# A hybrid decoder layer: rows normed per expert block, first loads of the attention issued in the front, and one row tile turned later

## What is computed

```python
mod = jax.nn.silu(c) @ w_ada[l] + b_ada[l]                  # shift, scale, gate, twice
u = x * (1.0 + sc1) + sh1
mix = token_mixer(u, w_in[l], w_conv[l], w_a[l], w_b[l], w_o[l])   # gated conv + stick-breaking attention, 8 heads
x = layer_norm(DN_ALPHA * x + g1 * mix, ln1_g[l], ln1_b[l])
u2 = x * (1.0 + sc2) + sh2
ffn = moe_ffn(u2, w_router, b_router, w_gate[l], w_up[l], w_down[l])   # 16 experts, each token goes to 2
x = layer_norm(DN_ALPHA * x + g2 * ffn, ln2_g[l], ln2_b[l])
```

## Time and profile before

| | value |
|---|---|
| runs, median of 3 (lowest, highest) | 2713.44 us (2708.99, 2715.66) |
| profiled execution, its own time | 2713.14 us |
| its span | 2711.5 us |
| PE, PEld busy | 2491.6 us (92%), 2081.0 us (77%) |
| DVE, ACT, POOL busy | 1443.4 us (53%), 1123.4 us (41%), 842.7 us (31%) |
| mean granted TensorE clock | 0.965 of 2.4 GHz |
| DMA | 548.04 MB, 202 GB/s over the span |
| chain of waits: gate and up products, down products of the experts | 16%, 8% of the span |

### The profile page before, as it was taken

How to read it: one execution, slowest core, us unless ns; L and a number is a source line. 1 busy time by engine, 2 the same in 40 slices (tenths; PEclk the granted TensorE clock), 3 DMA queues, 4 the chain that set the end, 5 groups by cost and what they waited for, 6 DMA issues and landing times. The chain is left out here.

```text
span 2711.5 us, 35984 instructions
## 1 busy us (share of the span) xinstructions
PE 2491.6 (92%) x12505; PEld 2081.0 (77%) x12506; DVE 1443.4 (53%) x1871; ACT 1123.4 (41%) x1846; POOL 842.7 (31%) x692
## 2 busy tenths in 40 slices
PE   5999899999999999999989989994998999999990
PEld 4788678778888888888878877884787888888780
DVE  6122156665656566665654335775446545534755
ACT  3122144554544444454542012212556545534754
POOL 2111023452222222222221345665322222322326
PEclk9999999999999999999999999996999999999995
DMA  7699676767575666585537666532567646555847
GB/s 265 232 312 314 250 231 189 250 199 233 184 224 165 227 186 218 173 270 183 171 122 239 213 182 210 187 117 108 164 180 228 207 135 204 169 145 146 266 122 263
DMA packets 258254, 548.04 MB, mean 202 GB/s; under 512 B 23716, under 2 KB 93464, under 8 KB 257496
## 3 DMA queue, kind: packets, MB, share of 16 engines
q1 hardware_dynamic: 236072, 483.07, 53.7%
q0 software_dynamic: 14720, 45.04, 7.6%
q10 hardware_dynamic: 7344, 18.35, 1.7%
HBM read 393.37 MB, written 153.02 MB: 202 GB/s over the span
## 5 line engine op out<-in xcount | busy, mean ns | idle before, releaser
L93 PE MATMUL mx_acc<-u_u,mx_w_hi 128*128 128x512 f32 x1792 | 571.4, 400 | 1.5 <-DMA mx_w_lo<-halves 1.5
L722 POOL TENSOR_TENSOR mx_wt<-mx_wt,mx_rest 128x127 f32<-128x127 f32 (+15 forms) x128 | 271.5, 2121 | 741.5 <-DVE mx_rest L924 741.5
L93 PEld LDWEIGHTS mx_acc<-u_u,mx_w_hi 128*128 128x128 f32 x1792 | 326.1, 190 | 65.9 <-DMA mx_w_lo<-halves 1.9
L932 DVE TENSOR_TENSOR mx_wt_lo<-mx_p_t,mx_wt_hi 128x512 fp32r<-128x512 f32 (+2 forms) x320 | 192.1, 604 | 326.4 <-ACT mx_wt_hi L887 324.5
L93 PE MATMUL mx_acc<-u_u,mx_w_lo 128*128 128x512 f32 x896 | 352.8, 394 | 0.0
L887 ACT ACTIVATE mx_wt_hi<-mx_p_t 128x512 fp32r<-128x512 f32 (+2 forms) x320 | 170.8, 534 | 405.4 <-PE mx_p_t L774 359.3
L924 DVE TENSOR_TENSOR_SCAN mx_rest<-mx_rest,mx_zero 128x128 f32<-128x128 f32 (+15 forms) x128 | 315.8, 2467 | 8.6 <-ACT mx_wt L869 8.6
L93 PE MATMUL moe_p_gu<-keep_wide_hi,moe_x_hi 128*128 128x512 f32 x656 | 262.6, 400 | 14.1 <-DVE keep_wide_lo L2043 13.0
L93 PE MATMUL moe_p_gu<-keep_wide_hi,moe_x_lo 128*128 128x512 f32 x656 | 258.1, 393 | 0.0
L93 PE MATMUL moe_p_gu<-keep_wide_lo,moe_x_hi 128*128 128x512 f32 x656 | 257.9, 393 | 0.0
L868 ACT ACTIVATE mx_rest<-mx_p_z 128x512 f32<-128x512 f32 (+2 forms) x320 | 171.0, 534 | 100.0 <-PE mx_p_z L761 58.9
(11 more groups left out here) (257 smaller groups left out, 5130.2 us busy)
## 6 DMA issues: line engine op xcount, KB each, us to landing
mx_w_hi<-halves SPq DMA_DIRECT2D x98, 512.0 KB, 3.8
mx_w_lo<-halves SPq DMA_DIRECT2D x98, 512.0 KB, 5.2
keep_stay<-in_w_gate SPq DMA_DIRECT2D x64, 512.0 KB, 5.3
keep_stay<-in_w_up SPq DMA_DIRECT2D x64, 512.0 KB, 6.4
keep_stay<-in_w_down SPq DMA_DIRECT2D x32, 1024.0 KB, 6.7
u_saved<-u_u SPq DMA_DIRECT2D x4, 4096.0 KB, 19.5
mx_w_mod<-in_w_ada SPq DMA_DIRECT2D x64, 256.0 KB, 5.2
gate_t<-mx_g_out SPq DMA_DIRECT2D x64, 256.0 KB, 5.1
```

Source lines behind the costliest of these rows:

```text
L93: mm = pe.matmul(out, a, b, start=first and n == 0, stop=last and n == len(pairs) - 1, skip_group_check=True)
L722: pool.tensor_tensor(wt[:, t % 2, 0:w - 1], wt[:, t % 2, 0:w - 1], rest[:, t % 2, 1:w], ALU.mult).then_inc(m["weights_done"], 1)
L932: dve.tensor_tensor(wt_lo[:, first:first + k - j], p_t[:, n % TR, 0:(k - j) * P].rearrange("p (j t) -> p j t", t=P), f32(wt_hi[:, first:fi ...
```

## The change

Three parts, independent of each other.

**1. The last norm goes into the expert loop.** Per block, the 128 rows of an earlier block are gathered from `acc` by POOL (`gather_rows`), centered by DVE (`center_rows`: two moments of 512 values each, their sum, subtraction of the mean with a product), scaled by ACT (`scale_rows`), given their bias by DVE (`add_bias`), and scattered to `out` by POOL (`store_rows`). Each token is in two blocks, so it is normed and stored twice, and the later store has both experts' contributions. The norm's row has its reciprocal root from POOL in `deviation`. SP's loads of `acc` and ACT's stores at the end are gone. Seven records are kept for five, moved by two copies of 128x12. At the start two blocks' iterations have a `load_clear` in place of the gathered rows; behind the last block the rows of the last three blocks are left.

**2. First loads in the front.** The places of the first head's keys, queries, values and two weight halves (`First`) now lie on front's x, stage and ring, and SP loads them within the front: keys at unit n = 38, queries and values at 39, the second queries at 40, the halves at 41 and 43, with the waits that free these places. The mixer's SP code begins with the remaining keys, two loads of w_ada's rows and the remaining values.

**3. First row tile turned later.** In the step t = 2 of the first norm `turn(0)` stands behind k = 6 and not behind k = 1. The other steps are unchanged.

```diff
+    def load_q(self, sp, n, qk_hi, qk_lo):
+        h, c = divmod(n, 4)
+        cols = slice(c * NB, (c + 1) * NB)
+        for half, src in enumerate((qk_hi, qk_lo)):
+            sp.dma_start(f32(self.q[half * HD:(half + 1) * HD, n % 2]), src[h * HD:(h + 1) * HD, cols]
+                         ).then_inc(self.q_in[n % 2], 16)
+
+    def load_k0(self, sp, h, qk_hi, qk_lo):
+        for half in range(2):
+            rows = slice(half * HD, (half + 1) * HD)
+            for dst, src in ((self.k0_hi, qk_hi), (self.k0_lo, qk_lo)):
+                sp.dma_start(f32(dst[rows, h % 2]), src[AW + h * HD:AW + (h + 1) * HD, 0:NB]
+                             ).then_inc(self.k0_in[h % 2], 16)
+
+    def load_v0(self, sp, h, v_tok):
+        sp.dma_start(f32(self.v0[:, h % 2]), v_tok.rearrange("(j p) h d -> p j h d", p=P)[:, 0:4, h]
+                     ).then_inc(self.v0_in[h % 2], 16)
+
+    def load_halves(self, sp, slot, n, halves):
+        for part, w in enumerate((self.w_hi, self.w_lo)):
+            sp.dma_start(f32(w[:, slot]).rearrange("p k n -> p (k n)"), halves[n, part]
+                         ).then_inc(self.halves_in[slot], 16)
+
```

In front, mixer and first norm:

```diff
+                if n == TB * UNITS - 10:
+                    sp.wait_ge(m["turned"], KD * TB)
+                    for i in range(2):
+                        sp.wait_ge(stored[i], 32 * UNITS)
+                    ahead_of.load_k0(sp, 0, qk_hi, qk_lo)
+                if n == TB * UNITS - 9:
+                    ahead_of.load_q(sp, 0, qk_hi, qk_lo)
+                    ahead_of.load_v0(sp, 0, v_tok)
+                if n == TB * UNITS - 8:
+                    ahead_of.load_q(sp, 1, qk_hi, qk_lo)
+                if n in (TB * UNITS - 7, TB * UNITS - 5):
+                    for i in range(2):
+                        sp.wait_ge(fill_kept[i], 32 * (FRONT_FILL // 2))
+                    slot = 0 if n == TB * UNITS - 7 else 1
+                    ahead_of.load_halves(sp, slot, slot, halves)
...
-            load_k0(0)
-            load_q(0)
-            load_halves(0)
+            load_k(0)
             load_mod(0)
-            load_q(1)
-            load_v0(0)
-            load_halves(1)
-            load_k(0)
             load_mod(1)
             load_v(0)
             for h in range(HEADS):
...
-                    if k == 1:
-                        if t - 3 in LATE_LOGITS:
-                            logits(t - 3)
+                    if k == 1 and t - 3 in LATE_LOGITS:
+                        logits(t - 3)
+                    if k == (KD - 2 if t == 2 else 1):
                         turn(t - 2)
```

GpSimd in the experts' stage (the iteration b with its waits, and the end):

```diff
@@ -1777,36 +1801,60 @@
                     else:
                         sp.wait_ge(m["dn_lo_done"], e * KF + (b - KD))
                     load_piece(sp, e, i, w_gate, w_up, w_down, stay, piece_in)
-            sp.wait_ge(m["gu_lo_done"], E * KD)
-            sp.wait_ge(m["dn_lo_done"], E * KF + KF)
-            sp.wait_ge(m["last_added"], 48)
-            for t in range(NT):
-                sp.dma_start(rows[:, t], acc[t * P:(t + 1) * P, :]).then_inc(rows_in[t], 16)
...
-                    wait_apart(pool, marks["pool"], m["record_ready"], 4 * n + (i + 1))
+                pool.tensor_copy(shifted[:], record[:, 1:SLOTS]).then_inc(m["record_step"], 1)
+                wait_apart(pool, marks["pool"], m["record_step"], n + 1)
+                pool.tensor_copy(record[:, 0:SLOTS - 1], shifted[:]).then_inc(m["record_ready"], 1)
+                wait_apart(pool, marks["pool"], m["record_ready"], n + 1)
...
+            def deviation(n):
+                wait_apart(pool, marks["pool"], m["row_mv"], n)
+                pool.tensor_scalar(var[:, 0:1], mv[:, 0, 1:2], EPS / ALPHA ** 2, None, ALU.add).then_inc(m["row_var"], 1)
+                wait_apart(pool, marks["pool"], m["row_var"], n)
+                pool.tensor_tensor(rstd[:, 0:1], var[:, 0:1], minus_half[:], ALU.pow).then_inc(m["row_rstd"], 1)
 
...
+                if n > 1:
+                    deviation(n - 1)
+                    load_clear(n - 1)
...
-
+            def block_rows(b, c=None):
+
+                if c is not None:
+                    wait_apart(pool, marks["pool"], m["normed"], b + 2)
+                    store_rows(0, row_out, m["out_stored"])
                 wait_apart(pool, marks["pool"], m["y_out"], b * 2 + 6)
-                add_rows(0, y, m["y_added"])
+                wait_apart(pool, marks["pool"], m["row_in"], b * 16 + 48)
+                add_rows(2, m["y_added"])
                 wait_apart(pool, marks["pool"], m["x_turned"], b + 4)
                 gather_x(b + 4)
+                if c is not None:
+                    wait_apart(pool, marks["pool"], m["out_stored"], c * 16 + 16)
+                pool.sem_inc(m["out_free"], 1)
+                deviation(b + 3)
                 wait_apart(pool, marks["pool"], m["y_added"], b * 16 + 16)
                 pool.sem_inc(m["y_free"], 1)
                 wait_apart(pool, marks["pool"], m["x_in"], b * 16 + 80)
                 shift_records(b + 4)
                 load_record(b + 5)
...
+                wait_apart(pool, marks["pool"], m["scaled"], b + 3)
+                gather_rows(1, row_in, m["row_in"])
+                record_known(b + 5)
+
+            block_rows(0)
+            block_rows(1)
+            with pool.Fori(0, total - 4) as c:
+                block_rows(c + 2, c)
+            wait_apart(pool, marks["pool"], m["normed"], total)
+            store_rows(0, row_out, m["last_stored"])
+            wait_apart(pool, marks["pool"], m["y_out"], total * 2 + 2)
+            wait_apart(pool, marks["pool"], m["row_in"], total * 16 + 16)
+            add_rows(2, m["last_added"])
+            pool.wait_ge(m["last_stored"], 16)
+            pool.sem_inc(m["out_free"], 1)
+            deviation(total + 1)
+            pool.wait_ge(m["last_added"], 16)
+            wait_apart(pool, marks["pool"], m["scaled"], total + 1)
+            gather_rows(2, row_in, m["row_in"])
+            gather_rows(3, last_in, m["last_row_in"])
+            wait_apart(pool, marks["pool"], m["normed"], total + 1)
+            store_rows(1, row_out, m["last_stored"])
+            deviation(total + 2)
+            pool.wait_ge(m["last_mv"], 1)
+            pool.tensor_scalar(var[:, 1:2], mv[:, 1, 1:2], EPS / ALPHA ** 2, None, ALU.add).then_inc(m["last_var"], 1)
+            pool.wait_ge(m["last_var"], 1)
+            pool.tensor_tensor(rstd[:, 1:2], var[:, 1:2], minus_half[:], ALU.pow).then_inc(m["last_rstd"], 1)
+            pool.wait_ge(m["last_stored"], 32)
+            pool.sem_inc(m["out_free"], 1)
+            wait_apart(pool, marks["pool"], m["normed"], total + 2)
+            store_rows(2, row_out, m["last_stored"])
+            pool.wait_ge(m["last_stored"], 48)
+            pool.wait_ge(m["last_normed"], 1)
+            store_rows(3, last_out, m["last_stored"])
+            pool.wait_ge(m["last_stored"], 64)
```

ScalarE and VectorE:

```diff
+            def scale_rows(n):
+                act.wait_ge(m["row_rstd"], n + 1)
+                act.wait_ge(m["centered"], n + 1)
+                act.wait_ge(m["out_free"], n + 1)
+                act.activation(row_out, row_in, ACT.Copy, scale=rstd[:, 0:1]).then_inc(m["scaled"], 1)
+
             def body(b, e, first):
                 high_h(b)
                 act.wait_ge(m["gu_used"], b * KD + 2 * KD)
                 for i in range(2):
                     act.activation(act_g[:, i * 256:(i + 1) * 256], p_gu[:, 0, i * 256:(i + 1) * 256], ACT.Silu
                                    ).then_inc(m["silu_done"], 1)
+                scale_rows(b)
                 high_x(b + 1)
...
+            def center_rows(n):
+                dve.wait_ge(m["row_in"], n * 16 + 16)
+                for i in range(2):
+                    dve.bn_stats(stats[:, 0, i], row_in[:, i * NB:(i + 1) * NB]).then_inc(m["row_stats"], 1)
+                wait_apart(dve, marks["dve"], m["row_stats"], 2 * n + 2)
+                dve.bn_aggr(mv[:, 0], stats[:, 0].rearrange("p a b -> p (a b)")).then_inc(m["row_mv"], 1)
+                dve.wait_ge(m["row_mv"], n + 1)
+                dve.scalar_tensor_tensor(out=row_in, in0=row_in, scalar=mv[:, 0, 0:1], in1=ln_g[:], op0=ALU.subtract,
+                                         op1=ALU.mult).then_inc(m["centered"], 1)
+
+            def add_bias(n):
+                dve.wait_ge(m["scaled"], n + 1)
+                dve.tensor_tensor(row_out, row_out, ln_b[:], ALU.add).then_inc(m["normed"], 1)
+
             def body(b, e, first):
                 low_h(b)
                 evict(b)
+                center_rows(b)
                 for i in range(2):
                     w = slice(i * 256, (i + 1) * 256)
                     dve.wait_ge(m["silu_done"], 2 * b + (i + 1))
                     dve.tensor_tensor(h[:, w], p_gu[:, 1, w], act_g[:, w], ALU.mult).then_inc(m["h_done"], 1)
                 low_x(b + 1)
+                add_bias(b)
                 if first:
```

240 lines of the change are left out of this document (91 added, 149 removed).

## The result

The changed kernel takes 2793.67 us (median of 4, 2793.28 to 2794.83) against 2713.78 us of before (median of 4), a ratio of 1.0296 with a 95% interval of 1.0284 to 1.0309: 80 us slower. The forecast was 2783, the range 2740 to 2850. The profiled execution has a span of 2793.1 us against 2711.5, so 81.6 us are to be found in the two traces.

A forecast was written before the change was run, and what follows sets the result against it. TensorE, busy 92% of the span, was taken as the bound, so only its idle stretches count. 23 + 60 + 11 + 14 - 26 - 7.1 - 5.4 = +69.5 us on 2713.14 gave 2783 us, range 2740 to 2850.

The forecast's parts named there:

- The chain: Plain block: turn, gather's issue, variance, power and scale precede x_hi, which starts 4.45 us later against 3.69 of slack.
- The changes: Twelve changes of expert: 3.3 us of idle TensorE plus 1.7 of slow clock each, +60 us (bounds 30 and 72).
- The three others: Three changes behind an expert of one block, where TensorE waits already: 3.6 us each, +11 us.
- the first two steps: Start of the expert loop: root also waits for gather's landing and moved records, +14 us (bounds 6 and 22).
- The plain blocks: 23 steps between blocks without change of expert or start: 1.0 us each, +23 us (bounds nothing and +46).
- the forecast case: Whole kernel: the summed terms, 2783 us, own range 2766 to 2800, chance 0.42.
- the rival of the long round: Expert loop: gathered rows land late, every block waits 2 us more, 80 above forecast less overlap, 2860 us; chance 0.15.
- my two signs of being wrong: Expert loop: x_hi starting within 3 us of the turn, or the block's period set by gathers of `acc`.
- The end: Behind the last blocks: tail norm mostly gone, -26 us (bounds -18 and -32).
- Front: Mixer's start: keys and queries already loaded, first product may begin at 330.6, -7.1 us (-4 to -10).
- First norm: Later `turn(0)`: its 5.72 us of idle is filled, -5.4 us (bounds -2 and -7).
- Contention of VectorE and GpSimd: Each block: centering or bias holds up GpSimd's root by 1.1 us, 44 in all less slack, 2823 us; chance 0.10.

The follow-up runs named there:

- front_turn: The kernel before with parts 2 and 3 of the change, without part 1: 2697.95 us, ratio 0.9950.
- turn_only: The kernel before with part 3 of the change alone: 2711.81 us, ratio 1.0001.
- root_early: The changed kernel with GpSimd's root (and the wait for the last scatter to `out`) ahead of its wait for the turn: 2763.75 us, ratio 1.0198.
- center_late: Changed kernel, scale behind x_hi or, at changes, the second high half (bias likewise), and centering behind h and x_lo except in experts' last blocks: 2743.98 us, ratio 1.0116.
- gather_early: The changed kernel with the gather of the norm's rows from `acc` issued ahead of the record copies and record load: 2843.74 us, ratio 1.0496.

## Why the prediction was right, point by point

- **The chain** behind the turn was as worked out: x_hi 3.97 us behind the turn, where I had 4.5. Of the rows I summed, only the waits were guessed, and too high by half a microsecond (the terms as written add to 2208.5, not 2208.4). For a plain block with its rows in time this left 0.34 us of loss and not 0.8, let alone 1.0.
- **The changes**: with the rows in time 2.81 us idle where I had 3.3, and behind five of these seven 1.4 to 2.9 us of slow clock, behind two none, 1.3 in the mean, where I had 1.7. The twelve came to 71 us and not to 60 because five of them also wait for late rows, which the forecast did not have there. The three others took 9.6 (11), the first two steps 15.0 (14).
- **The plain blocks**: 26 us for 23, nearly as forecast, but of other parts. 17 of them cost 6.6 together, where 17 were forecast; six wait for late rows and cost 19.7, where 6 were.
- **Late rows are the term that the forecast case left out.** They were the rival of the long round, priced 2 us a block for all 40 blocks; the rows came late in eleven blocks, each the second of its expert, and what they cost came on top of the forecast case, not in its place. I had set the two as alternatives, where they add. If these eleven steps had cost what the others of their kind did, the loop would be 36 us shorter, an estimate from the table of steps. Of my two signs of being wrong, x_hi within 3 us of the turn did not show; a period set by the gathers of `acc` did, for these eleven steps of 40.
- **The end**: -28.7 (forecast -26).
- **Front**: `front_turn` and `turn_only` leave 14 us for it (in the profiled executions 9 to 11), where I had 7.1. The first product gained 5.07, two less than forecast: the barrier came 0.9 later, and GpSimd's copy of the identity ends 1.2 us behind the mixer's first load, which I hadn't looked at. But I had missed a second stall of before: its mixer's SP code issues the other keys (L595) behind fourteen other loads, and TensorE waits for them (timeline of before, a row that I hadn't read):

```profile
354.60 0.19 PEld L760 LDWEIGHTS mx_p_z<-mx_k_hi,mx_q 128*128 128x128 f32 x1 [5.15 <-DMA mx_k_lo<-qk_lo]
```

  In after those keys are the first loads of the mixer, and this wait (4.71 us for the product) is gone.
- **First norm**: a step that failed. I had -5.4 with bounds of -2 and -7; measured is -1.2 by the medians (within 0.1% of nothing), as the logits wait 3.18 us. I had named that wait and then left it at almost nothing; the row that sets it, ScalarE's copy behind its scale of the next row tile, does not move with the turn.
- **Contention of VectorE and GpSimd.** In after the root is mostly computed while VectorE has no such instruction, and the variance takes 0.28 (two take 1.20), so the rival that had it as a cost in each block did not come. In `root_early`, where it falls beside the centering, it takes 1.19 (timeline):

```profile
2284.47 1.28 DVE L2125 SCALAR_TENSOR_TENSOR keep_stay<-keep_stay,moe_mv,moe_ln_g 128x1024 f32<-128x1024 f32 x1
2284.65 1.19 POOL L1844 TENSOR_SCALAR moe_var<-moe_mv 128x1 f32<-128x1 f32 x1
```

  That is the rule of the Trainium skill that the prediction weighed ("SBUF — State Buffer", section "Who interferes with whom"), for a subtraction with a product whose rows and weights both lie in SBUF; the variance ends 0.1 us behind the centering. It cost hardly anything in after, and may have cost some of what the early root might have won.

The total came right within 11 us, and that was partly luck. In the loop the forecast case by itself was about 22 us too dear (an estimate: all 12 changes and 23 others at the price of those whose rows came in time give some 86 us, where 108 was forecast), and the late rows that it left out brought 36. By the traces front and end together gained 6 more than forecast, and the first norm 4 less.

## What to carry to other kernels

Work that is moved from a tail into a loop beside a busy engine is free only if no instruction of it stands ahead of one that the busy engine waits for; ask of each inserted instruction what it waits for, not how long it takes. Here the scale takes 1.15 us and cost 58 in the loop by where it stood. And a chain of transfers with waits has a round of its own: add it up from landing to landing in the worst block, not the typical one, before a wait in it is moved earlier, since the wait that is removed may have been the one that ran beside the others.

## What the runs showed of the hardware that was not expected

- Idle stretches of TensorE of almost the same length had different consequences for the clock. Behind 2.81 us at one change of after the next 48 matmuls took 12.83 us, behind 2.83 us at another 11.18, the full clock. Of the waits of about 2 us some left a slow stretch as well (1.97 us: 12.79; 2.20 us: 11.17); the granted clock was 0.71 in the 3.5 us behind the first of these and 1.00 in the 3.1 us behind the second. The length of the gap alone does not decide.
- A gather or scatter of 128 rows of 4 KB costs GpSimd 1.0 us (scatter-add 1.6) to issue. Until the step that waits for it could run, 4.2 us went by from the gather of x in a quiet block of after (2491.63 to 2495.82), 6.0 in center_late (2176.25 to 2182.24) and 7.0 from the scatter-add in gather_early. Four of them and one record load came to a round of 18.9 us in the block of center_late beside the loads of weights, and of 19.3 in gather_early, where their waits stood one behind the other.
